# An expert's input matrix loaded in two transfers of 1.5 MB in place of four of 768 KB, with four neighbouring rows on a partition in place of two

## The reference, cut to what matters

```
probs = softmax(t @ router_w + router_b)          # 16 experts in 4 groups, top 2 within the best group
for e in range(N_EXPERTS):
    gu = t @ w_in[e]                               # (512, 1024) @ (1024, 768)
    act = jax.nn.silu(gu[:, :D_EXPERT]) * gu[:, D_EXPERT:]
    y = y + gates[:, e:e + 1] * (act @ w_out[e])   # (512, 384) @ (384, 1024)
```

## Time and profile before

| | |
|---|---|
| time, median of 3 runs | 1994.57 us (1988.2 to 1995.43) |
| the profiled execution's own time | 1990.73 us |
| its span, first to last instruction | 1988.5 us |
| mean granted TensorE clock | 0.865 of full speed |
| TensorE busy | 1568.2 us, 79% of the span |
| DVE, ACT, POOL busy | 915.6, 681.6, 149.3 us |
| loads of the input matrices | 128 transfers of 768 KB, median 6.1 us from issue to landing |

### The profile page before, as it was taken

One profiled execution on the slowest core, in us unless ns is written; L12 is line 12 of the kernel. 1 busy time (PEld: TensorE's weight loads), 2 busy tenths in 40 slices (PEclk: granted clock), 3 DMA queues, 4 the chain that ended last, 5 costly groups with the idle time before them and its releaser, 6 DMA issues. The chain is left out here.

```text
span 1988.5 us, 18936 instructions
## 1 busy us (share of the span) xinstructions
PE 1568.2 (79%) x7369; PEld 1265.8 (64%) x7369; DVE 915.6 (46%) x1317; ACT 681.6 (34%) x1066; POOL 149.3 (8%) x162
## 2 busy tenths in 40 slices
PE   5991799476698784799983899879698784799983
PEld 4881766355576563687863787768576563687862
DVE  3214456544354435466644324542254435466643
ACT  3211134312243423455532325131243423455530
POOL 0001000100000000111110002240000000111110
PEclk8995558657899897799996899889899897799996
DMA  4324000001242025699963242213142015699963
GB/s 138 96 68 75 2 1 1 2 1 49 74 156 88 0 84 199 221 354 356 350 239 113 96 156 66 85 43 102 63 155 88 0 43 199 224 351 352 360 239 149
DMA packets 108874, 270.22 MB, mean 136 GB/s; under 512 B 40417, under 2 KB 43122, under 8 KB 104434
## 3 DMA queue, kind: packets, MB, share of 16 engines
q1 hardware_dynamic: 93810, 200.84, 29.6%
q10 hardware_dynamic: 5472, 51.38, 6.9%
q0 software_dynamic: 9504, 16.80, 2.2%
HBM read 263.68 MB, written 23.07 MB: 144 GB/s over the span
## 5 line engine op out<-in xcount | busy, mean ns | idle before, releaser
L185 DVE TENSOR_TENSOR w_lo<-w_stage,w_hi 128x2048 fp32r<-128x2048 f32 (+2 forms) x74 | 171.4, 2326 | 414.5 <-ACT w_hi L175 414.5
L175 ACT ACTIVATE w_hi<-w_stage 128x2048 fp32r<-128x2048 f32 (+2 forms) x74 | 135.9, 1847 | 473.7 <-PE bank L214 375.6
L2107 PE MATMUL bank<-e_wo,e_actT 128*128 128x512 f32 x384 | 170.4, 593 | 3.5 <-ACT e_actT L2169 3.5
L1997 DVE TENSOR_TENSOR e_wi_lo<-e_wi,w_hi 128x1536 fp32r<-128x1536 f32 x60 | 105.5, 1758 | 64.6 <-ACT w_hi L1993 64.6
L2107 PEld LDWEIGHTS bank<-e_wo,e_actT 128*128 128x128 f32 x384 | 72.2, 190 | 80.7 <-issue 78.9
L1997 DVE TENSOR_TENSOR e_wi_lo<-e_wi,w_lo 128x1536 fp32r<-128x1536 f32 x60 | 105.4, 1757 | 17.9 <-ACT w_lo L1993 17.9
L1993 ACT ACTIVATE w_hi<-e_wi 128x1536 fp32r<-128x1536 f32 x60 | 89.1, 1488 | 56.5 <-PE bank L2096 50.7
L1993 ACT ACTIVATE w_lo<-e_wi 128x1536 fp32r<-128x1536 f32 x60 | 89.0, 1483 | 17.2 <-PE bank L2096 17.2
L2096 PE MATMUL bank<-e_wi_lo,e_hx_hi 128*128 128x384 f32 x256 | 88.0, 344 | 0.0
L2095 PE MATMUL bank<-e_wi_lo,e_hx_hi 128*128 128x384 f32 x256 | 87.9, 343 | 0.0
L2229 DVE TENSOR_TENSOR e_hx_lo<-bank,e_hx_hi 128x512 fp32r<-128x512 f32 x68 | 43.8, 686 | 64.2 <-ACT e_hx_hi L2162 64.2
(11 more groups left out here) (472 smaller groups left out, 3848.5 us busy)
## 6 DMA issues: line engine op xcount, KB each, us to landing
e_wi<-in_moe_w_in SPq DMA_DIRECT2D x128, 768.0 KB, 6.1
e_wo<-in_moe_w_out ACTq DMA_DIRECT2D x30, 1536.0 KB, 9.1
w_stage<-in_x_wkv SPq DMA_DIRECT2D x16, 1024.0 KB, 5.1
w_stage<-in_sg_w_in SPq DMA_DIRECT2D x16, 1024.0 KB, 5.3
w_stage<-in_hyb_w_in SPq DMA_DIRECT2D x10, 1024.0 KB, 5.1
w_stage<-in_x_wq SPq DMA_DIRECT2D x8, 1024.0 KB, 6.3
w_stage<-in_x_wo SPq DMA_DIRECT2D x8, 1024.0 KB, 5.1
w_stage<-in_sg_w_out SPq DMA_DIRECT2D x8, 1024.0 KB, 5.0
```

The costliest lines, as they stand in the source:

```text
L175: act.activation(self.w_hi[h][:, :, :cols], self.stage[h][:, :, :cols], ACT.Copy)\
L185: dve.tensor_tensor(self.w_lo[h][:, :, :cols], self.stage[h][:, :, :cols], self.w_hi[h][:, :, :cols], ALU.subtract).then_inc(self.lo_done[ ...
L1997: dve.tensor_tensor(self.lo[q][:, :, :], self.raw[q][:, :, :], self.hi[q], ALU.subtract).then_inc(self.wi_los[q], 1)
L2107: ins = pe.matmul(y_ps[n][:, :], auT[:, f, :], wo[j][:, f, n * GC:(n + 1) * GC], start=f == 0, stop=f == CO - 1)
```

## The change

The four buffers `raw[q]` become halves of two larger ones, `half[h]`, each with four neighbouring rows (12 KB) on a partition. An expert's input matrix is loaded by two transfers of 1.5 MB. Each of them waits for the `lo` of both quarters that it overwrites. `hi` of quarters 0 and 1 waits for the landing of half 0, that of quarters 2 and 3 for half 1. The transposes of the tokens take every fourth feature of a range of 512 (16 bytes apart) in place of every second of 256. Sizes of `hi`, `lo` and of the products are as before.

```
-        self.raw = [m.sb(c, f"{nm}_wi{q}", [P, KC, 2 * DE]) for q in range(CI)]
+        self.half = [m.sb(c, f"{nm}_wi{h}", [P, 2 * KC, 2 * DE]) for h in range(2)]
+        self.raw = [self.half[q // 2][:, q % 2 * KC:(q % 2 + 1) * KC, :] for q in range(CI)]
...
     def load_in(self, sp, e, n):
-        for q in range(self.CI):
+        rows = 2 * self.KC * P
+        for h in range(2):
             if n:
-                sp.wait_ge(self.wi_los[q], n)
-            sp.dma_start(self.raw[q][:, :, :], self.w_in[e * D + q * self.KC * P:e * D + (q + 1) * self.KC * P, :]
-                         .rearrange("(p k) n -> p k n", p=P)).then_inc(self.wi_in[q], 16)
+                sp.wait_ge(self.wi_los[2 * h], n)
+                sp.wait_ge(self.wi_los[2 * h + 1], n)
+            sp.dma_start(self.half[h][:, :, :], self.w_in[e * D + h * rows:e * D + (h + 1) * rows, :]
+                         .rearrange("(p k) n -> p k n", p=P)).then_inc(self.wi_in[h], 16)
...
     def split_hi(self, act, n, q):
-        act.wait_ge(self.wi_in[q], 16 * (n + 1))
+        act.wait_ge(self.wi_in[q // 2], 16 * (n + 1))
...
                 def turn_tokens(j):
                     for k in range(KD):
                         ins = pe.transpose(turn_ps[k // 4][:, (k % 4) * P:(k % 4 + 1) * P],
-                                           hx[:, j, k // KC * KC * P + k % KC:(k // KC + 1) * KC * P:KC], m.ident[:, :])
+                                           hx[:, j, k // 4 * 4 * P + k % 4:(k // 4 + 1) * 4 * P:4], m.ident[:, :])
```

More of the change, by code:

```diff
@@ L1973, in __init__ @@
         self.tok = m.sb(c, f"{nm}_tok", [P, T, D])
-        self.wi_in, self.wi_his, self.wi_los = ([m.sem(f"{nm}_wi_{s}{q}") for q in range(CI)] for s in ("in", "hi", "lo"))
+        self.wi_in = [m.sem(f"{nm}_wi_in{h}") for h in range(2)]
+        self.wi_his, self.wi_los = ([m.sem(f"{nm}_wi_{s}{q}") for q in range(CI)] for s in ("hi", "lo"))
         self.wo_in = [m.sem(f"{nm}_wo_in{j}") for j in range(2)]
@@ L2042, in _ @@
                     e = expert(sp, i)
[L2043 to L2046, removed]
+                    for h in range(2):
+                        sp.wait_ge(w.wi_los[2 * h], i + L)
+                        sp.wait_ge(w.wi_los[2 * h + 1], i + L)
+                        sp.dma_start(w.half[h][:, :, :], w.w_in[bass.ds(e * D + h * 2 * KC * P, 2 * KC * P), :]
+                                     .rearrange("(p k) n -> p k n", p=P)).then_inc(w.wi_in[h], 16)
             @block.gpsimd
@@ L2212, in _ @@
                         act.wait_ge(wi_used[q], i + L)
-                        act.wait_ge(w.wi_in[q], i * 16 + 16 * NE)
+                        act.wait_ge(w.wi_in[q // 2], i * 16 + 16 * NE)
                         act.activation(w.hi[q], w.raw[q][:, :, :], ACT.Copy).then_inc(w.wi_his[q], 1)
```

## The result

The changed kernel takes 2002.57 us in the median of six runs (1997.16 to 2009.19), the kernel before 1992.39 (1988.2 to 1995.43); the ratio is 1.0053, 95% interval 1.003 to 1.0076. Measured a second time it was 2004.14 us and 1.0064 (1.0041 to 1.0088). It is slower by 10 to 11 us, where 2.2 us and no visible change were forecast.

What follows compares the result with a forecast made beforehand. TensorE, busy 148.50 of 148.50 us over ten steps, was taken to bound the steps. Steps 0, front 2 x 1.1 and transposes 0 gave +2.2 us on the mean of 1992.2: 1994.4 us, range 1987 to 2004.

Steps and rivals of the forecast that it cites:

- The bound of a step: Expert loop steps: TensorE is busy throughout, 14.85 us a step, so changed transfers can cost time but give none.
- faster: Rival 3: fewer, larger transfers carry more GB/s, gaining at most 1 us a layer in the front; over 0.5% faster, chance 0.03.
- the landing of half 1: Expert loop steps: half 1 lands by 873.5 to 875.7, 1.2 to 3.4 us to spare; no wait, cost 0.
- the upper bound that I set aside: Steps: if halves took `e_wo`'s 9.8 us, half 0 would be 0.35 us and half 1 0.71 us too late.
- The path of the wait: Steps: a late half makes `hi` wait, and `lo` and TensorE's next product behind it.
- Rival 2: Steps: half 0 or 1 lands too late for `hi`; 0.7 us in some 26 steps, +18 us, 2012 us; chance 0.04.
- The front: Second expert's load before the loop: 768 KB more beside the gathers delays the barrier, 1.1 us twice, +2.2 us, bounds 0 and +4.4.
- The transposes: Token transposes, 272 in TensorE's full steps: reading with a step of 16 bytes costs 0, bounds -3 and +32 us.
- First expert: Front: half 0 lands later, ACT starts 0.9 us later, idle time absorbs it; 0, from -0.2 to +1 us a layer.
- SP's queue: SP in the steps and run-time loop: two issues fewer per expert, effect 0.
- within 0.5%: Whole kernel: time not visibly changed, chance 0.86, including the main forecast of 0 to +4.4 us at 0.74.

Runs made afterwards that it cites:

- the changed kernel without the front's part: Changed kernel with half 1 of the second expert loaded behind the barrier at the start of the expert loop: 2000.77 us, 1.004 of the kernel before.
- the kernels in which only the front's part is left: Changed kernel with only half 1 whole (1.0013), `silu` ahead of `hi` of quarter 2 (1.0014), or `e_wo` issued behind next step's `hi` of quarter 0 (1.0016) or 2 (1.0018).
- the row layout alone: Changed kernel's four rows on a partition and transposes, but each quarter loaded, asked for and awaited by itself: 1993.47 us, 1.0002 of the kernel before.
- silu moved: Changed kernel with `silu` ahead of `hi` of quarter 2 on ACT and the multiply ahead of `lo` of quarter 2 on DVE: 1997.68 us, 1.0014.

## Why the prediction was wrong

**The bound of a step: right.** TensorE had no idle time to give, and the change could only cost. So "faster" was rightly left at 0.03.

**The step that failed: the landing of half 1.** I wrote that it needs "two quarters more, 4.4 us" after half 0, lands by 873.5 to 875.7, 5.7 to 7.9 us after its issue, with 1.2 to 3.4 us to spare, and took no wait at all. Measured: in the same step half 0 was in at 862.40 + 7.1 = 869.5 us, as forecast (869.1 to 871.3). Half 1, issued at 866.96, was ready for `hi` at 877.24, 10.2 us after its issue and 7.7 after half 0, and over 840 to 1009 us it takes up to 13.1 us against 9.09 available. So the term of 4.4 us is the one that failed. At 873.0 only 0.23 MB were missing, by my estimate 0.65 us at the 354 GB/s of the steps and within the forecast; they took 4.2 us, while `e_wo` had 78.8% of the engines. That half 1 "shares the engines with `e_wo`" I had named and then not counted. The step back was missing as well: a late `hi` makes the next request late, and then `e_wo` stands ahead of half 1. Each part alone is harmless: half 1 whole behind early quarters gives 1.0013, half 0 whole gives 1.0, `e_wo` later gives 1.0016. The nearest row was the upper bound that I set aside: `e_wo` itself, 1.5 MB in the same traffic, 9.0 to 9.8 us, and even that was too low.

**The path of the wait: named wrongly.** Rival 2, at 0.04, was the one that came, and I had it reach TensorE through `lo` and the next product. It reaches it through `silu`, which stands behind the waiting `hi` on ACT; with `silu` ahead of it the loss in the steps is gone. The rival's price of 18 us was worked out from 0.7 us a step lost in full; in truth waits of 3.8 us a step are mostly absorbed, and only the long ones pass. What the steps cost by time is the changed kernel without the front's part: 0.4% of 1992.33 us, 8 us (0.25 to 0.55%). The traces of single executions show from 3.9 to 16.6 us; why one execution has more long waits than another stays open.

**The front: right mechanism, too small.** Foreseen was 1.1 us a layer with bounds 0 and 2.2. The profile shows 1.5 us in layer 0 and 1.7 in layer 1. The timed price is in the kernels in which only the front's part is left, 1.0013 to 1.0018: 2.6 to 3.6 us for both layers, within +4.4. The parts add up within their intervals: 0.0040 and 0.0014 make 0.0054, against 0.0053 and 0.0064 for the whole.

**The transposes: right.** A step of 16 bytes has 1 ns more in the interval, and the row layout alone is at 1.0002. The rule of the Trainium skill (SBUF — State Buffer, section Door 1: The DMA port swizzle), by which one read per line should pay, is not borne out for this operand: the trace has 120 ns, where the prediction's estimate by lines gave 119 + 22 = 141.

**First expert, SP's queue: no sign against them.** The parts above already add up to the whole. They weren't tested by themselves, and the intervals leave room for 1 or 2 us.

**The range held by luck.** 2002.57 us lies within 1987 to 2004, the second measurement of 2004.14 just outside. But the upper end was made of gathers, slower transposes and a run at the upper end, not of a late half 1; and 0.86 stood on "within 0.5%", 0.04 on the rival that came.

Open: whether 12 KB on a partition in one transfer adds or saves anything by itself. With 6 KB and the same waits the loss was no smaller (1.0078), so the size isn't its cause.

## What to carry to other kernels

When two transfers become one, the request moves to the later of the two free moments and the landing to the later of the two ends; lay the new landing by the nearest row of the new size in the same traffic, not by the old size plus a remainder, and count every other transfer that is asked for before it ends. Ask too whether the waiting instruction frees the buffer of the next request: then a wait comes back a step later. Then look at what stands behind the waiting instruction on its engine: an unrelated `silu` behind a `hi` that could wait cost 0.4%. In this kernel 768 KB more, issued just ahead of a barrier, cost 1.5 to 1.7 us through the gathers that the barrier waits for.

## What the runs showed of the hardware

A transfer engine share of 0.96 went with a TensorE that never waited, and a share of 0.93 both with one that waited (changed kernel) and with one that didn't (silu moved): here the share didn't tell what sets the pace. 1.5 MB landed after 6.5 us alone (`e_wo`) and after up to 13.1 us in the steps of the changed kernel (half 1). Of two transfers of 1.5 MB on two queues, asked for 1.4 us apart, the last 0.23 MB of the first took 4.2 us, while the second moved 1.35 MB. Gathers beside 768 KB more landed 1.6 us later (7.2 in place of 5.6 us), beside 768 KB less 0.4 us earlier. In these traces the weight load of a 128 x 128 transpose takes 140 ns with neighbouring elements and 207, 199 and 213 ns with steps of 8, 12 and 16 bytes: being strided costs, how far, up to 16 bytes, hardly matters.
